# A two-block layer kernel: layer-norm work of the first stage grouped together, weight streams divided differently, and mix parts put ahead of bank drains

## What is computed

```python
def gmlp_mixer(u, v, ln_g, ln_b, w_s, b_s):      # u, v after GELU
    vn = layer_norm(v, ln_g, ln_b).reshape(B, n_chunks, 128, 4, 256)
    w = w_s * jnp.tril(...)
    mixed = jnp.einsum('gts,bnsgd->bntgd', w, vn) + b_s.T[None, None, :, :, None]
    return u * mixed.reshape(B, S, GMLP_WIDTH)
...
def rwkv7_mixer(h, mu_prev, mu_next, w_r, w_k, w_v, ...):
    dx_p = shift_right(h) - h
    dx_n = shift_left(h) - h
    def mix(c):
        return h + dx_p * mu_prev[c] + dx_n * mu_next[c]
    xw, xa, xg = mix(1), mix(4), mix(5)           # narrow products
    r, k, v = mix(0) @ w_r, mix(2) @ w_k, mix(3) @ w_v   # wide products
    ...
```

## Time and profile before

| | |
|---|---|
| median of 3 runs | 3103.1 us (3102.56 to 3107.66) |
| the profiled execution | 3103.1 us, span 3101.4 us |
| TensorE matmul busy | 2894.7 us, 93% of the span |
| DVE busy | 1481.2 us, 48% |
| ACT busy | 1240.7 us, 40% |
| POOL busy | 450.7 us, 15% |
| mean granted TensorE clock | 0.972 |

### The profile page before, as it was taken

The page is one execution under the profiler, slowest core; times in us unless marked ns, Lnnn a source line. Parts: engine busy times, 40 slices in busy tenths (PEclk is TensorE's granted clock), DMA queues, the critical chain, the costliest instruction groups (busy, mean ns, idle before and its releaser), DMA issues. The chain is left out here.

```text
span 3101.4 us, 56635 instructions
## 1 busy us (share of the span) xinstructions
PE 2894.7 (93%) x24856; PEld 2335.4 (75%) x24856; DVE 1481.2 (48%) x2292; ACT 1240.7 (40%) x2077; POOL 450.7 (15%) x343
## 2 busy tenths in 40 slices
PE   7999999699989999898889999897999999889999
PEld 5877557588868888775578887676888888678887
DVE  2533766533453333536553344965555555453343
ACT  3322654422242222325443233654455554443232
POOL 1001550100000000113100000003344444100000
PEclk9999999799999999999999999998999999999999
DMA  4212002223213222232122222220000000322221
GB/s 167 87 68 82 1 1 77 94 95 109 95 69 122 89 97 104 81 118 63 65 96 95 95 98 79 103 82 15 6 7 7 7 5 5 125 81 103 95 95 68
DMA packets 38821, 228.84 MB, mean 74 GB/s; under 512 B 4352, under 2 KB 8448, under 8 KB 15024
## 3 DMA queue, kind: packets, MB, share of 16 engines
q1 hardware_dynamic: 32576, 201.34, 18.1%
q0 software_dynamic: 6000, 23.87, 2.3%
HBM read 220.93 MB, written 4.26 MB: 73 GB/s over the span
## 5 line engine op out<-in xcount | busy, mean ns | idle before, releaser
L431 DVE TENSOR_TENSOR weights_lo<-ring,weights_hi 128x1024 fp32r<-128x1024 f32 x344 | 425.4, 1238 | 700.3 <-ACT weights_hi L424 700.2
L424 ACT ACTIVATE weights_hi<-ring 128x1024 fp32r<-128x1024 f32 x364 | 381.8, 1053 | 596.6 <-PE bank L561 360.5
L480 PE MATMUL bank<-h_hi,weights_hi 128*128 128x512 f32 x512 | 204.6, 400 | 33.6 <-DVE weights_lo L431 23.8
L481 PE MATMUL bank<-h_lo,weights_hi 128*128 128x512 f32 x512 | 203.1, 397 | 0.0
L482 PE MATMUL bank<-h_hi,weights_lo 128*128 128x512 f32 x512 | 202.8, 396 | 0.0
L480 PE MATMUL bank<-mlp_h_hi,weights_hi 128*128 128x512 f32 x512 | 200.9, 392 | 2.0 <-DVE mlp_h_lo L776 2.0
L481 PE MATMUL bank<-mlp_h_lo,weights_hi 128*128 128x512 f32 x512 | 200.6, 392 | 0.0
L482 PE MATMUL bank<-mlp_h_hi,weights_lo 128*128 128x512 f32 x512 | 200.2, 391 | 0.0
L559 PE MATMUL bank<-weights_hi,mlp_p_hi 128*128 128x512 f32 x512 | 199.4, 389 | 0.0
L561 PE MATMUL bank<-weights_hi,mlp_p_lo 128*128 128x512 f32 x512 | 199.2, 389 | 0.0
L560 PE MATMUL bank<-weights_lo,mlp_p_hi 128*128 128x512 f32 x512 | 199.2, 389 | 0.0
(11 more groups left out here) (487 smaller groups left out, 6266.4 us busy)
## 6 DMA issues: line engine op xcount, KB each, us to landing
ring<-in_w_m SPq DMA_DIRECT2D x64, 1024.0 KB, 4.6
ring<-in_w_mb SPq DMA_DIRECT2D x24, 1024.0 KB, 4.5
ring<-in_w_fi SPq DMA_DIRECT2D x22, 1024.0 KB, 4.6
ring<-in_w_fo SPq DMA_DIRECT2D x10, 1024.0 KB, 4.8
ring<-in_w_a SPq DMA_DIRECT2D x7, 1024.0 KB, 4.8
attn_bias<-scratch POOLq DMA_DIRECT2D x16, 448.0 KB, 4.7
ring<-in_w_rg SPq DMA_DIRECT2D x5, 1024.0 KB, 4.8
ring<-in_w_v SPq DMA_DIRECT2D x4, 1024.0 KB, 15.2
```

Source lines behind the costliest of these rows:

```text
L424: act.e.activation(halves(g, s)[0], raw, ACT.Copy).then_inc(*act.up("act_unit_high", ("high", s)))
L431: lane.e.tensor_tensor(lo, raw, hi.bitcast(F32), ALU.subtract).then_inc(*lane.up(f"{lane.name}_unit_low", ("low", s)))
L480: pe.e.matmul(ps[:, :], hi, xh, start=k == 0, stop=False, skip_group_check=True)
L481: pe.e.matmul(ps[:, :], hi, xl, start=False, stop=False, skip_group_check=True)
```

## The change

In the front stage the layer norm is taken tile by tile: DVE runs mean, subtraction, reciprocal and both full-width operations of a tile before it begins the next, and waits for that tile's deviation in between; ACT runs Square and square root for each tile. Both do all four tiles before their loops over w_u. The stream group of w_v and w_u now ends with w_u: units 0 to 2 of w_q are no longer made in the loops over w_u, but behind the fence, high halves by ACT and low halves by POOL behind its transfers and settings. In the RWKV input stage ACT's step i makes the high part of wide block i ahead of `act_wide_block(i-1)`, and in step 7 the first three small high parts ahead of it as well; DVE makes the low part of wide block i-1 ahead of `low_unit` instead of behind it.

```diff
--- before.py
+++ after.py
@@ -43,7 +43,7 @@
 ATT_SLOTS = 16
 
 RAW = ("wk1", "wv1")
-GROUPS = (("w_v", "w_u", "w_q", "w_kv"), ("w_vt",), ("w_xr", "w_rg"), ("w_mb0", "w_mb1", "w_mb2", "w_o"),
+GROUPS = (("w_v", "w_u"), ("w_q", "w_kv"), ("w_vt",), ("w_xr", "w_rg"), ("w_mb0", "w_mb1", "w_mb2", "w_o"),
           ("w_fi0", "w_fo0", "w_fi1", "w_fo1"), ("w_a2",), ("w_va",), ("w_ao",), ("w_m100", "w_m200", "w_m101", "w_m201"),
           ("w_rr", "w_rw", "w_rk", "w_ra", "w_rv", "w_rg1"), ("w_ro",), ("w_m110", "w_m210", "w_m111", "w_m211"))
 STREAM = [("w_v", 8192), ("w_u", 8192), ("w_q", 8192), ("w_kv", 8192), ("wk1", 4096), ("wv1", 4096),
@@ -836,20 +836,19 @@
         act.e.activation(L.V[:, qt, half * 512:half * 512 + 512], filled(g, act, ("w_v", i))[:, :], ACT.Gelu_apprx_tanh,
                          accum_out=L.row_sums[:, 2 * qt + half:2 * qt + half + 1]).then_inc(
             *act.up("act_v", ("v", i), ("drained", ("w_v", i))))
+    for qt in range(QT):
+        act.wait_ge(g.at("centred", qt))
+        act.wait_ge(act.newest)
+        act.e.activation(L.sqs, L.V[:, qt, :], ACT.Square, accum_out=L.st[:, qt, 1:2]).then_inc(*act.up("act_ln"))
+        act.wait_ge(act.newest)
+        act.e.activation(L.st[:, qt, 2:3], L.st[:, qt, 1:2], ACT.Sqrt, scale=1.0 / D, bias=g.eps[:, 0:1]).then_inc(
+            *act.up("act_ln", ("deviation", qt)))
     for what, i in gemm_steps("w_u", NB, range(NB)):
         if what == "unit":
             act_unit(g, act, i)
             continue
         act.e.activation(L.uT[:, i, :], filled(g, act, ("w_u", i))[:, :], ACT.Gelu_apprx_tanh).then_inc(
             *act.up("act_u", ("u", i), ("drained", ("w_u", i))))
-        if i < QT:
-            act.wait_ge(g.at("centred", i))
-            act.wait_ge(act.newest)
-            act.e.activation(L.sqs, L.V[:, i, :], ACT.Square, accum_out=L.st[:, i, 1:2]).then_inc(*act.up("act_ln"))
-        if i == QT - 1:
-            act.wait_ge(act.newest)
-            act.e.activation(L.st[:, :, 2], L.st[:, :, 1], ACT.Sqrt, scale=1.0 / D, bias=g.eps[:, 0:1]).then_inc(
-                *act.up("act_ln", ("deviations",)))
     end(g, act, "front")
 
 
@@ -870,28 +869,24 @@
         for qt in range(QT):
             dve.wait_ge(g.at("v", (half, qt)))
     dve.wait_ge(g.at("ln_consts"))
-    sums = L.row_sums.rearrange("p (q n) -> p n q", n=2)
-    dve.e.tensor_tensor(st[:, :, 0], sums[:, 0], sums[:, 1], ALU.add).then_inc(*dve.up("dve_ln"))
-    dve.wait_ge(dve.newest)
-    dve.e.tensor_scalar(st[:, :, 0], st[:, :, 0], 1.0 / D, None, ALU.mult).then_inc(*dve.up("dve_ln"))
-    dve.wait_ge(dve.newest)
     for qt in range(QT):
+        dve.e.tensor_tensor(st[:, qt, 0:1], L.row_sums[:, 2 * qt:2 * qt + 1], L.row_sums[:, 2 * qt + 1:2 * qt + 2],
+                            ALU.add).then_inc(*dve.up("dve_ln"))
+        dve.wait_ge(dve.newest)
+        dve.e.tensor_scalar(st[:, qt, 0:1], st[:, qt, 0:1], 1.0 / D, None, ALU.mult).then_inc(*dve.up("dve_ln"))
+        dve.wait_ge(dve.newest)
         dve.e.tensor_scalar(L.V[:, qt, :], L.V[:, qt, :], st[:, qt, 0:1], None, ALU.subtract).then_inc(
             *dve.up("dve_ln", ("centred", qt)))
+        dve.wait_ge(g.at("deviation", qt))
+        dve.e.reciprocal(st[:, qt, 3:4], st[:, qt, 2:3]).then_inc(*dve.up("dve_ln"))
+        dve.wait_ge(dve.newest)
+        dve.e.scalar_tensor_tensor(L.V[:, qt, :], L.V[:, qt, :], st[:, qt, 3:4], L.lng, ALU.mult, ALU.mult).then_inc(
+            *dve.up("dve_ln"))
+        dve.wait_ge(dve.newest)
+        dve.e.tensor_tensor(L.V[:, qt, :], L.V[:, qt, :], L.lnb, ALU.add).then_inc(*dve.up("dve_ln", ("ln", qt)))
     for what, i in gemm_steps("w_u", NB, range(NB)):
         if what == "unit":
             low_unit(g, dve, i)
-            continue
-        if i == QT - 1:
-            dve.wait_ge(g.at("deviations"))
-            dve.e.reciprocal(st[:, :, 3], st[:, :, 2]).then_inc(*dve.up("dve_ln"))
-            dve.wait_ge(dve.newest)
-        if i >= QT:
-            qt = i - QT
-            dve.e.scalar_tensor_tensor(L.V[:, qt, :], L.V[:, qt, :], st[:, qt, 3:4], L.lng, ALU.mult, ALU.mult).then_inc(
-                *dve.up("dve_ln"))
-            dve.wait_ge(dve.newest)
-            dve.e.tensor_tensor(L.V[:, qt, :], L.V[:, qt, :], L.lnb, ALU.add).then_inc(*dve.up("dve_ln", ("ln", qt)))
     for fb in range(NB):
         dve.wait_ge(g.at("u", fb))
         ps = filled(g, dve, ("mixed", fb))
@@ -966,6 +961,8 @@
 def act_nsa_in(g, act):
     L = g.L1
     fence(g, act, "front")
+    for s in first_units("w_q"):
+        act_unit(g, act, s)
     for what, i in gemm_steps("w_q", NB, range(NB)):
         if what == "unit":
             act_unit(g, act, i)
@@ -1023,6 +1020,8 @@
     pool.wait_ge(pool.newest)
     for q, name in ((L.kc2, "pe_k"), (L.vc2, "pe_v")):
         pool.e.tensor_copy(q[:, 4, 0:32:2], g.vec[name]).then_inc(*pool.up("pool_positions", ("positions",)))
+    for s in first_units("w_q"):
+        low_unit(g, pool, s)
     for s in first_units("w_vt"):
         low_unit(g, pool, s)
     end(g, pool, "nsa_in")
@@ -2304,14 +2303,15 @@
         for i in range(NB):
             if i + 1 < NB:
                 act_mix_owns(g, act, c, i + 1)
+            if wide is not None:
+                act_mix_high(g, act, wide, i)
+            if i == NB - 1:
+                for k in range(3):
+                    act_mix_high(g, act, small, k)
             if i:
                 act_wide_block(g, act, c, i - 1)
                 if c == 3:
                     early(first, i - 1)
-            if wide is not None:
-                act_mix_high(g, act, wide, i)
-        for k in range(3):
-            act_mix_high(g, act, small, k)
         act_wide_block(g, act, c, NB - 1)
         if c == 3:
             early(first, NB - 1)
@@ -2346,15 +2346,13 @@
                 dve_mix_sum(g, dve, small, i)
             if wide is not None and i < NB:
                 dve_mix_sum(g, dve, wide, i)
+            if wide is not None and i:
+                dve_mix_low(g, dve, wide, i - 1)
             if i == NB:
-                if wide is not None:
-                    dve_mix_low(g, dve, wide, NB - 1)
                 for k in range(3):
                     dve_mix_low(g, dve, small, k)
             if i and wide_unit(name, i - 1) is not None:
                 low_unit(g, dve, wide_unit(name, i - 1))
-            if wide is not None and 0 < i < NB:
-                dve_mix_low(g, dve, wide, i - 1)
             if c == 3 and i == 0:
                 dve_scan_set(g, dve)
             if c == 3 and i:
```

## The result

The changed kernel takes 3153.9 us in the median of 4 runs (3150.43 to 3156.46) against 3103.94 us, ratio 1.016 with a 95% interval from 1.0147 to 1.0172. The profiled execution took 3153.24 us, with a span of 3151.5 us, 50.1 more than the 3101.4 before. The forecast was 3155.6.

What follows compares the result with a forecast made beforehand. TensorE, busy for 93% of the span, bounds the kernel. Stalls of 11.0 + 11.4 + 12.5 + 9.2 = 44.1 us, plus 10.4 for four restarts, less 2.0, add 52.5 to 3103.1: 3155.6 us, range 3146 to 3164.

Steps and rivals of the forecast that it cites:

- The norm's chain: Front: the norm's four tiles, 5.4 us each, on DVE and ACT delay block 3 of w_u by 11.0 us.
- Rival (c): ACT switches tables at each Square and each root, six more switches of 1.30 us: 3163.4 us; chance 0.05.
- rival (b): Front is covered, only RWKV pays, as the norm's chain stays under 13.3 us: 3128.0 us; chance 0.03.
- The clock: TensorE runs partly at 1.2 GHz behind each long stall: 2.6 us for each of four restarts, 10.4 us.
- The start of w_q: Front: w_q waits for fence and POOL, starting 18.4 us behind the mixed matmuls instead of 7.06: 11.4 us added.
- T: Start of the mixed matmuls in the front, forecast at 133.0 instead of 119.38.
- Rounds 0 and 2: RWKV input: DVE's step grows from 4.64 to 6.26 us; narrow products start 12.5 and 9.2 us late.
- given back: RWKV input: waits inside the two narrow products partly vanish, taken as 2.0 us, possibly 0 to 3.7.
- The bound of 3.7: RWKV input: most that waits inside narrow products could return, 5.8 us less the 2.1 ahead of the first.
- Rival (a): TensorE is far enough ahead in the RWKV rounds, so only the front pays: 3130.7 us; chance 0.05.
- (d): Earlier low parts end 5.8 us of waits ahead of and inside narrow products, nothing stalls: 3097.3 us; chance 0.02.
- (e): No change that can be told, as all stalls in both stages are covered; chance 0.02.

Runs made afterwards that it cites:

- norm alone: The kernel before with only the layer norm taken tile by tile: 3119.12 us against 3102.88, ratio 1.0052.
- DVE's units: The changed kernel with the low halves of w_q's first three units on DVE instead of POOL: 3152.07 us against 3104.92 for the kernel before, ratio 1.0149.
- ACT's order: The kernel before with only ACT's new order in the RWKV rounds, DVE's as before: 3131.06 us against 3102.88, ratio 1.0091.
- group alone: The kernel before with only the stream group cut behind w_u, w_q's first three units made behind the fence: 3113.72 us against 3102.88, ratio 1.0041.
- DVE's order: The kernel before with only DVE's new order in the RWKV rounds, ACT's as before: 3102.58 us against 3104.92, ratio 0.9991.
- RWKV rounds alone: The kernel before with only the new orders of both ACT and DVE in the RWKV rounds: 3121.83 us against 3102.88, ratio 1.0056.
- tiles overlapped: The changed kernel with the norm's four means and subtractions ahead of all waits for a deviation: 3146.3 us against 3104.92 for the kernel before, ratio 1.013.
- gate weights early: The kernel before with both halves of the gate weights made ahead of the loops over w_kv: 3097.04 us against 3104.92, ratio 0.9979.
- The faster version: The kernel before with the early gate split and small mix parts reordered at the end of RWKV rounds 0 and 2: 3096.18 us against 3104.27, ratio 0.9977.

## Why the prediction was right, point by point

**The norm's chain.** Forecast 11.0 us for block 3; the start moved by 10.6, the wait is 10.72. A tile took 5.33 us where the sum has 5.4 (98.52 less 93.19, the starts of two reciprocals). Only two table loads stand in the chain, at the first root and at the first u drain, and each took 1.3 us, as in the earlier trace rows. The Trainium skill, ScalarE: Activation LUTs, section What ACT_TABLE_LOAD costs, gives 2.66 us for a switch, by which block 3 would have started an estimated 2.7 us later than it did: here the measurement decides against the page. Rival (c) fell with the two loads, and rival (b) with the chain's 22.7 us (78.56 to 101.26), against a cover of 13.3, and with the wait ahead of w_q.

**The clock.** 2.6 us for each restart: between block 3 and the mixed matmuls 30.15 us instead of 27.21, so 2.9; with the norm alone 28.98, so 1.8; behind the start of w_q 2.4, up to the gate matmuls. In the 10 us behind block 3 the granted clock was 0.70, and 0.73 in the earlier trace rows. The size varies from run to run around what was taken; why is open.

**The start of w_q.** T was 132.9 (forecast 133.0), though this hides 0.4 us too much for the chain and 0.3 too little for the clock. w_q started 18.5 us behind it (18.4), so 11.5 us were added there; the sum has 11.4, and its own terms make 11.3. POOL's transfers and settings are 4.2 us of that (144.77, the end of DVE's drains, to 148.96); the run with DVE's units agrees.

**Rounds 0 and 2.** Step 6.25 (6.26). The narrow product of round 0 came 12.4 us late (12.5). In round 2 DVE's chain from its last sum of step 1 to the narrow product took 43.8 us (2053.16 to 2096.96), forecast 44.0. Yet up to the third narrow product only 10.9 us were added, where the sum has 9.2 and two restarts less 2.0, 12.4. The term that was mis-sized is what the two slowed narrow products cost, restarts less what is given back: 3.2 us forecast, 1.9 measured. DVE's last sum of step 1 in round 2 ends 16.85 us behind the start of round 0's narrow product instead of 15.68, which is 1.2 us, and behind the narrow product of round 2 another 0.7 us are added. The matmuls that start 0.43 us apart there instead of 0.227 cost 2.2 and 2.5 us, so 2.8 us were given back, not 2.0. Of these, 2.1 are the waits of 0.62 and 1.49 us inside the two products, both gone; what the rest is, is open. The bound of 3.7 was too wide, as it counts two waits of round 3 that stayed.

Rival (a) fell: three units split ahead did not cover blocks 3 to 7, nor the narrow product, whose operands come last in DVE's round. Rivals (d) and (e) fell with the steps of 6.25 us, longer than a block of 5.44. Why ACT's order is the cause, and DVE's is not, is shown by the two runs of one order alone.

**Round 3** was forecast at nothing; its two short waits are 0.46 and 1.12 us, as before.

Sum: front 27.6 forecast, 27.4 measured to the gate matmuls; 0.9 less in the code between the stages; RWKV 24.9 forecast, 23.3 measured; behind it 0.2. So the 52.5 us added were 2.4 too many by the profiles and 2.5 by the medians. That the time itself was only 1.7 us too high is luck by 0.8 us: the kernel before had a median of 3103.9 in the comparison, not the 3103.1 that the sum starts from.

## What to carry to other kernels

Count cover in the busy engine's blocks from the moment at which the first missing operand is ready, and then walk the in-order queues of the other two engines up to that operand: each instruction put ahead of it counts in full, and a wait inside that queue counts as much as work. If two engines wait for each other within one iteration, what each does while the other waits is added to the step; putting independent work ahead of the wait took 8 of 10.7 us off in the norm. First operands made behind a fence cost the fence, everything that the engine's program does ahead of them, and the clock of the restart; making them in the stage before cost no wait here, as the buffers allowed it.

## What the runs showed that was not expected

The same code of the scan took 557.7 us from its first heads to the output product in the kernel before (2124.61 to 2682.34), and 562.6 us with the norm alone (2136.38 to 2699.01). The rows show a granted clock below full at its end there, and full in the kernel before; the windows give busy us (count) of PE, PEld, DVE, ACT and POOL, the clock, and the DMA share and GB/s:

```profile
2640.00:2690.00 50.00, 41.25 (x908) 33.79 (x904) 19.79 (x46) 24.51 (x33) 11.54 (x9) 1.00 0.26 96
```

```profile
2650.00:2700.00 50.00, 41.47 (x944) 34.13 (x943) 16.80 (x45) 19.31 (x28) 7.51 (x5) 0.90 0.16 50
```

Nothing in the two programs differs in that part. A clock of 0.90 over 50 us means 10 us at the lower level of 1.2 GHz, or 5 us of full clock lost, which is the size of the difference. The other profiles agree, each read in its last 50 us ahead of the output product:

| granted clock | scan, us | kernels |
|---|---|---|
| 1.00 | 557.3 to 557.9 | before, changed, group alone, ACT's order, DVE's order |
| 0.93 | 560.2 | RWKV rounds alone, tiles overlapped, DVE's units |
| 0.90 | 562.3 and 562.6 | gate weights early, norm alone |

The faster version took 555.2 us at 1.00, with 9 us less at the lower level in the scan as a whole. So clock and length go together in all eleven profiles; no run set the clock by itself, and what decides whether it falls there was not settled. The kernel before and the changed one were profiled at the same level, so their 50 us are free of it. It is why single parts here are judged by starts within their stage as well as by the whole time.
